# A two-layer decoder step on one core: a fifth row buffer, sample V products over all heads, an operand in PSUM, and attention's preparation moved

## The reference

```python
def swa_sample(xn, ck, cv, w_qkv, b_qkv, w_o, b_o, sinks):
    q, k, v = qkv_proj(xn, w_qkv, b_qkv, qpos)          # with rotary
    kk = jnp.concatenate([ck, k], axis=1)
    vv = jnp.concatenate([cv, v], axis=1)
    o = attend(q, kk, vv, mask, sinks)                  # w = p / denom; o = w @ v
    return o @ w_o + b_o, kk[:, -rows:], vv[:, -rows:]
...
x = x + mixer(rmsnorm(x)); x = x + hier_moe(rmsnorm(x))
...
bbar_r = coef_r * br - coef_i * bi                      # s5_mix, per group of channels
bbar_i = coef_r * bi + coef_i * br
```

## Time and profile before

| | before |
|---|---|
| timed runs, median | 990.99 us (990.83 to 991.28, 3 runs) |
| profiled execution: its time, its span | 988.24, 986.5 |
| mean granted clock of TensorE | 0.866 |
| busy in the span: TensorE, VectorE | 747.4 (76%), 415.8 (42%) |
| busy in the span: ScalarE, GpSimd | 260.2 (26%), 153.5 (16%) |

### The profile page before, as it was taken

How to read it: one execution, slowest core, us unless ns; L and a number is a source line. 1 busy time by engine, 2 the same in 40 slices (tenths; PEclk the granted TensorE clock), 3 DMA queues, 4 the chain that set the end, 5 groups by cost and what they waited for, 6 DMA issues and landing times.

```text
span 986.5 us, 12287 instructions
## 1 busy us (share of the span) xinstructions
PE 747.4 (76%) x4643; PEld 451.5 (46%) x4643; DVE 415.8 (42%) x1002; ACT 260.2 (26%) x554; POOL 153.5 (16%) x218
## 2 busy tenths in 40 slices
PE   4899948999899535998740369989999935998640
PEld 2344426758545333554420257644445524555420
DVE  3478684827578751211115485701111252111118
ACT  6120016616111101332112145520023321222113
POOL 1010000000796401332110112000000001232110
PEclk9999977959999756999985589989999955999995
DMA  9461117000504495999949566592040192999946
GB/s 347 138 197 57 48 59 252 2 1 2 190 21 171 165 401 220 405 410 408 398 137 409 107 127 184 110 364 101 1 170 22 56 390 91 400 410 410 403 161 239
DMA packets 74803, 201.77 MB, mean 205 GB/s; under 512 B 14808, under 2 KB 29528, under 8 KB 73688
## 3 DMA queue, kind: packets, MB, share of 16 engines
q1 hardware_dynamic: 57784, 161.77, 45.4%
q0 software_dynamic: 9696, 19.75, 5.8%
q10 hardware_dynamic: 7264, 19.46, 5.3%
HBM read 171.64 MB, written 39.39 MB: 214 GB/s over the span
## 4 chain that ended last, share of the span: by engine, by line
PE 52%; DVE 15%; DMA 14%; SPq 8%; ACT 6%; issue 4%; POOL 0%; PEldq 0%; POOLq 0%; DVEq 0%; ACTq 0%; PEld 0%
PE PSUM L1995 13%; PE PSUM L1592 9%; PE PSUM L1803 8%; SPq L459 5%; DMA XNT<-in_moe_w_up 4%; DMA PH<-y_scratch 3%; PE PSUM L1823 3%; DMA RING<-in_attn_w_qkv 2%; PE PSUM L1791 2%; SPq L465 2%; PE PSUM L1673 2%; DVE XNT L734 2%; PE PSUM L1945 2%; PE PSUM L1941 2%; DVE X L1475 2%
## 5 line engine op out<-in xcount | busy, mean ns | idle before, releaser
L1592 PE MATMUL PSUM<-RING,XNT 128*128 128x512 f32 (+2 forms) x256 | 94.5, 567 | 4.1 <-DMA RING<-in_attn_w_qkv 3.4
L632 POOL DMA_INDIRECT PH<-xn_scratch,PH x32 | 32.6, 1020 | 359.0 <-DVEq L1420 249.6
L1995 PE MATMUL PSUM<-PH,XNT 128*128 128x512 f32 (+1 forms) x220 | 88.1, 593 | 0.3 <-PE PSUM L1995 0.3
L1803 PE MATMUL PSUM<-RING,PH 128*64 128x256 f32 x384 | 74.9, 417 | 13.2 <-DMA PH<-in_moe_w_up 6.5
L1803 PE MATMUL PSUM<-PH 128*64 128x256 f32 x384 | 65.3, 402 | 10.8 <-DMA RING<-in_moe_w_up 6.2
L1451 DVE TENSOR_TENSOR PH<-PH,PSUM 128x128 f32<-128x128 f32 x32 | 9.3, 289 | 148.8 <-ACT PH L937 148.8
L1592 PEld LDWEIGHTS PSUM<-RING,XNT 128*128 128x128 f32 (+1 forms) x256 | 40.4, 177 | 53.7 <-issue 47.7
L1750 PE MATMUL PSUM<-RING,PH 128*128 128x512 f32 (+1 forms) x160 | 62.6, 593 | 0.0
L1803 PEld LDWEIGHTS PSUM<-RING,PH 128*64 128x64 f32 x384 | 44.4, 151 | 35.1 <-issue 19.8
L708 ACT ACTIVATE XNT<-X 128x1024 f32<-128x1024 f32 (+1 forms) x25 | 26.4, 1054 | 122.0 <-DVE X L1333 66.4
L1995 PEld LDWEIGHTS PSUM<-PH,XNT 128*128 128x128 f32 (+1 forms) x220 | 36.3, 179 | 47.6 <-issue 47.5
(11 more groups left out here) (371 smaller groups left out, 1360.1 us busy)
## 6 DMA issues: line engine op xcount, KB each, us to landing
RING<-in_moe_w_gate SPq DMA_DIRECT2D x24, 512.0 KB
RING<-in_moe_w_up SPq DMA_DIRECT2D x24, 512.0 KB
PH<-in_moe_w_gate SPq DMA_DIRECT2D x24, 512.0 KB
PH<-in_moe_w_up SPq DMA_DIRECT2D x24, 512.0 KB
RING<-in_moe_w_down SPq DMA_DIRECT2D x24, 512.0 KB
PH<-in_moe_w_down SPq DMA_DIRECT2D x24, 512.0 KB
XNT<-in_moe_w_gate SPq DMA_DIRECT2D x16, 512.0 KB
XNT<-in_moe_w_up SPq DMA_DIRECT2D x16, 512.0 KB
```

What stands on the lines that cost most here:

```text
L632: pool.indirect_dma_start(out=XG[:, i % 2, :], out_offset=None, in_=xn_d[layer], in_offset=bass.IndirectOffsetOnAxis(ap=IDX[:, i:i + 1], a ...
L1592: last = te.matmul(PSUM[lo:hi, b0 + col // 512, col % 512:col % 512 + n], XT[:, c, t * P:t * P + r], RING[:, c // 2, (c % 2) * QKV + col:( ...
L1803: last = te.matmul(PSUM[m * 64:(m + 1) * 64, 2 + i % 2, 0:2 * FF], XGT[:, i % 2, c, m * 64:(m + 1) * 64], gu[:, :, c, :], start=(c == 0), ...
L1995: last = te.matmul(PSUM[p0:p0 + r, 2 * (i % 2) + w, :], XT[:, c, t * P:t * P + r], slot(SLOT[q])[:, (2 * (c % 3) + w) * 512:(2 * (c % 3) + ...
```

## The change

1. The K cache's transposes and copies move from phase 2 to phase 1, into the last tile's turn, ahead of its wait for the rotation. `v_block(7)` comes before the last rotation. `inputs()` moves from VectorE to GpSimd, after phase 1; SyncE stores its result behind the `w_o` loads. VectorE's wait before attention is for the V blocks' stores alone.
2. Sample V products: per sample one instruction over all four heads' probabilities and 256 columns of V (and one for the new tokens), of which `out_scale` takes the heads' own blocks, in 8 products of 32 partitions. They fill banks 6 and 7, and `pv` waits for one scaling more at and behind a sample unit.
3. W blocks: half of BB is copied to PSUM bank 3, twice, and four of the six products read it there. VectorE waits for ScalarE's fourth copy of O first. Blocks come 3, 2, 2, 1, 0 to a tile.
4. `YG` gets a fifth buffer: `rows_back` issues five reads with no wait between; the block loads follow. The coefficient and state loads go before the last expert pairs are done, instead of after. `xn_stored` is one semaphore.

The diff leaves out the moved tiles' places in SBUF, `xn_stored`, and the removal of VectorE's `inputs()`, whose body stands in GpSimd's program now.

```diff
@@ -392,10 +390,6 @@
                              ).then_inc(S(f"vec_out{k % 2}"), 16)
-            sp.wait_ge(S("bb_ready"), 1)
-            sp.dma_start(in_d[:, 0:2 * GP * CH], BBQ.rearrange("p r g c -> p (r g c)")).then_inc(S("bb_out"), 16)
-            sp.dma_start(in_d[:, 2 * GP * CH:], PWRQ.rearrange("p r k g -> p (r k g)")).then_inc(S("bb_out"), 16)
-
...
@@ -489,23 +483,24 @@
                 for t in range(NT):
-                    if layer == 0 and t == 4:
-                        for k in range(4):
-                            ring_load(Q_SSM + k, [(slot(SLOT[Q_SSM + k])[:, 0:BLK_F], blk_d[k])])
-                    if t >= 4:
-                        sp.wait_ge(S("yg_used"), layer * 2 * NT + 2 * (t - 3))
-                    sp.dma_start(YG[t % 4][0:ROWS[t], :, :],
+                    sp.dma_start(YG[t][0:ROWS[t], :, :],
                                  y_d[layer].rearrange("(k n) d -> n k d", k=2)[t * P:t * P + ROWS[t]]
-                                 ).then_inc(S(f"yg_full{t % 4}"), 16)
-
+                                 ).then_inc(S(f"yg_full{t}"), 16)
+
+            sp.wait_ge(S("bb_ready"), 1)
+            sp.dma_start(in_d[:, 0:2 * GP * CH], BBQ.rearrange("p r g c -> p (r g c)")).then_inc(S("bb_out"), 16)
+            sp.dma_start(in_d[:, 2 * GP * CH:], PWRQ.rearrange("p r k g -> p (r k g)")).then_inc(S("bb_out"), 16)
             experts(0)
-            sp.wait_ge(S("ring_free"), Q_SSM)
+            sp.wait_ge(S("ring_free"), Q_M0 + 28)
             sp.dma_start(INS, in_d).then_inc(S("ins_in"), 16)
+            sp.wait_ge(S("ring_free"), Q_M0 + 30)
             for r, src in enumerate((st_re, st_im)):
...
             rows_back(0)
+            for k in range(4):
+                ring_load(Q_SSM + k, [(slot(SLOT[Q_SSM + k])[:, 0:BLK_F], blk_d[k])])
...
@@ -576,7 +571,18 @@
             end_phase(pool, 1)
-
+            pool.wait_ge(S("b_in"), 16 * 4)
+            for k in range(8):
+                pool.tensor_copy(PWRQ[:, :, k, :], PW[:, :, 7 - k, :])
+            pool.tensor_copy(PWRQ[:, :, 8, :], PW[:, :, 8, :])
+            cf = [bc(CF[:, r, :].unsqueeze(2), [P, GP, CH]) for r in range(2)]
+            pool.tensor_tensor(BT1, cf[0], BBI[:, 0], ALU.mult)
+            ch(pool.tensor_tensor(BT2, cf[1], BBI[:, 1], ALU.mult))
+            ch(pool.tensor_tensor(BBQ[:, 0], BT1, BT2, ALU.subtract))
+            pool.tensor_tensor(BT1, cf[0], BBI[:, 1], ALU.mult)
+            ch(pool.tensor_tensor(BT2, cf[1], BBI[:, 0], ALU.mult))
+            ch(pool.tensor_tensor(BBQ[:, 1], BT1, BT2, ALU.add))
+            pool.sem_inc(S("bb_ready"), 1)
...
@@ -838,6 +844,11 @@
             for t in range(NT):
+                if t == 4:
+                    for i in range(NSEQ):
+                        act.wait_ge(S("ck_transposed"), i + 1)
+                        nc.scalar.activation(KCT[:, i, :, :], PSUM[0:64, 4 + i % 2, :].rearrange("p (h k) -> p h k", h=KVH),
+                                             ACT.Copy).then_inc(S("kct_ready"), 1)
...
@@ -861,11 +872,6 @@
             end_phase(act, 1)
-
-            for i in range(NSEQ):
-                act.wait_ge(S("ck_transposed"), i + 1)
-                nc.scalar.activation(KCT[:, i, :, :], PSUM[0:64, 4 + i % 2, :].rearrange("p (h k) -> p h k", h=KVH),
-                                     ACT.Copy).then_inc(S("kct_ready"), 1)
...
@@ -1200,11 +1194,11 @@
                     powers()
-                for k in {0: (0, 1), 1: (2, 3), 2: (4, 5), 3: (6,), 4: (7,)}[t]:
+                for k in {0: (0, 1), 1: (2, 3), 2: (4, 5), 3: (6, 7), 4: ()}[t]:
                     v_block(k)
-            inputs()
             end_phase(dve, 1)
-            dve.wait_ge(S("bb_out"), 32)
+            for b in range(2):
+                dve.wait_ge(S(f"vec_out{b}"), 16 * NB // 2)
...
@@ -1281,8 +1275,11 @@
                 else:
-                    for e in range(2):
-                        ins = ve.tensor_tensor(OD[b][:, :, e * 64:(e + 1) * 64], ps, bc(rd, [P, 4, HD]), ALU.mult)
+                    for hh in range(KVH):
+                        rows = slice(32 * hh, 32 * hh + 32)
+                        own = PSUM[rows, 6:8, :].rearrange("p b (g n) -> p (b g) n", g=2)[:, :, hh * HD:(hh + 1) * HD]
+                        for e in range(2):
+                            ins = ve.tensor_tensor(OD[b][rows, :, e * 64:(e + 1) * 64], own, bc(rd[rows], [32, 4, HD]), ALU.mult)
...
@@ -1313,7 +1310,11 @@
                 pw = [bc(PWRW[:, r, 0:L, g0:g0 + BP].rearrange("p k g -> p g k").unsqueeze(3), [P, BP, L, CH]) for r in range(2)]
-                bv = [bc(BBW[:, r, g0:g0 + BP, :].unsqueeze(2), [P, BP, L, CH]) for r in range(2)]
+                half = PSUM[:, 3, :].rearrange("p (r g c) -> p r g c", r=2, g=GP // 2)
+                if k % 4 == 0:
+                    ch(ve.tensor_copy(half, BBW[:, :, g0:g0 + GP // 2, :]))
+                h0 = g0 % (GP // 2)
+                bv = [bc(half[:, r, h0:h0 + BP, :].unsqueeze(2), [P, BP, L, CH]) for r in range(2)]
...
@@ -1321,10 +1322,10 @@
             dve.wait_ge(S("ins_in"), 16)
+            dve.wait_ge(S("ot_ready"), 4)
             for t in range(NT):
-                if t < 4:
-                    w_block(2 * t)
-                    w_block(2 * t + 1)
+                for k in {0: (0, 1, 2), 1: (3, 4), 2: (5, 6), 3: (7,), 4: ()}[t]:
+                    w_block(k)
...
@@ -1470,9 +1471,9 @@
-                    dve.wait_ge(S(f"yg_full{t % 4}"), 16 * (layer * (2 if t % 4 == 0 else 1) + t // 4 + 1))
+                    dve.wait_ge(S(f"yg_full{t}"), 16 * (layer + 1))
                     for k in range(2):
-                        ve.scalar_tensor_tensor(out=X[0:r, t, :], in0=YG[t % 4][0:r, k, :], scalar=CW[0:r, t, k:k + 1],
+                        ve.scalar_tensor_tensor(out=X[0:r, t, :], in0=YG[t][0:r, k, :], scalar=CW[0:r, t, k:k + 1],
...
@@ -1609,6 +1610,15 @@
                     rr = ROWS[tt]
+                    if tt == 4:
+                        pe.wait_ge(S("qkv_read"), 4)
+                        pe.wait_ge(S("ck_in"), 16)
+                        for i in range(NSEQ):
+                            if i >= 2:
+                                pe.wait_ge(S("kct_ready"), i - 1)
+                            for h in range(KVH):
+                                last = te.transpose(PSUM[0:64, 4 + i % 2, h * P:(h + 1) * P], CK[:, i, h * 64:(h + 1) * 64], IDENT[:, :])
+                            last.then_inc(S("ck_transposed"), 1)
...
@@ -1678,7 +1688,9 @@
                 pe.wait_ge(S("pt_ready_act"), i + 1)
-                if i >= 2:
+                if kind == "s" or i and UNITS[i - 1][0] == "s":
+                    pe.wait_ge(S("o_scaled"), i)
+                elif i >= 2:
...
@@ -1691,23 +1703,13 @@
                         sq = 4 * b + g
-                        for hh in range(KVH):
-                            o = PSUM[32 * hh:32 * hh + 32, 6 + i % 2, g * 64:(g + 1) * 64]
-                            te.matmul(o, pt[:, g, 0, 32 * hh:32 * hh + 32], VC[:, sq, hh * 64:(hh + 1) * 64],
-                                      start=True, stop=False)
-                            last = te.matmul(o, pt[0:64, g, 1, 32 * hh:32 * hh + 32], V[0:64, 4, hh * 64:(hh + 1) * 64],
-                                             start=False, stop=True)
+                        o = PSUM[:, 6 + g // 2, (g % 2) * KVD:(g % 2 + 1) * KVD]
+                        te.matmul(o, pt[:, g, 0, :], VC[:, sq, :], start=True, stop=False)
+                        last = te.matmul(o, pt[0:64, g, 1, :], V[0:64, 4, :], start=False, stop=True)
                 last.then_inc(S("pv_done"), 1)
             scores(0)
             scores(1)
-            pe.wait_ge(S("ck_in"), 16)
-            for i in range(NSEQ):
-                if i >= 2:
-                    pe.wait_ge(S("kct_ready"), i - 1)
-                for h in range(KVH):
-                    last = te.transpose(PSUM[0:64, 4 + i % 2, h * P:(h + 1) * P], CK[:, i, h * 64:(h + 1) * 64], IDENT[:, :])
-                last.then_inc(S("ck_transposed"), 1)
             pe.wait_ge(S("kct_ready"), NSEQ)
             pe.wait_ge(S("vc_in"), 16)
             for i in range(NU):

```

More of the change, by code:

```diff
@@ L258, in build @@
         YG1 = XTF[:, 0:4 * D].rearrange("p (b n) -> p b n", b=4)
-        YG = [(YG0 if t < 2 else YG1)[:, 2 * (t % 2):2 * (t % 2) + 2, :] for t in range(4)]
+        YG = [(YG0 if t < 2 else YG1)[:, 2 * (t % 2):2 * (t % 2) + 2, :] for t in range(4)] + [YB]
         RF = RING.rearrange("p k n -> p (k n)")
@@ L453, in experts @@
                         if e == RS + XS + 1:
[L454 removed]
+                            sp.wait_ge(S("xn_stored"), 16 * NT * (layer + 1))
                         if freed(q):
@@ L625, in moe @@
                 pool.wait_ge(S("routed"), layer + 1)
-                pool.wait_ge(S(f"xn_stored{layer}"), 16 * NT)
+                pool.wait_ge(S("xn_stored"), 16 * NT * (layer + 1))
                 n0 = PAIRS * layer
```

26 lines of the change are left out of this document (6 added, 20 removed).

## The result

| | before | changed |
|---|---|---|
| timed runs, median | 990.91 (985.48 to 991.28) | 953.61 (949.2 to 963.55), 4 runs |
| timed again beside other kernels | 988.57 (986.33 to 994.08) | 953.87 (948.07 to 956.43), 4 runs |
| ratio to the runs of before | | 0.9621 [0.9567, 0.9675]; again 0.9635 [0.9595, 0.9675] |
| profiled execution, span | 986.5 | 954.1 |

The kernel is faster, by 35 to 37 us; 948 was forecast, in a range of 939 to 964. Timed runs of either kernel lie 6 to 8 apart. Of the 7.7 between the two traces of the changed kernel 1.4 lie before the first exponential, 1.0 in attention and 6.6 behind GpSimd's copy of the RING rows; the stretches between are 1.3 shorter.

What follows compares the result with a forecast made beforehand. No engine was taken to bound the kernel everywhere; each edit was priced in its stage. 11.3 + 14 + 13 + 4.5 = 42.8 took the profiled time from 988.24 to 945.4; with 2.75 to the timed median, 948, range 939 to 964.

Steps and rivals of the forecast that it cites:

- A: Attention's preparation moved beside the last rotation: unit 0's exponential comes earlier, a gain of 11.3 (9 to 11.8).
- B: Output projection: W blocks with an operand in PSUM relieve VectorE and GpSimd, routing starts earlier; gain 13 (5.6 to 14).
- The rival of no relief: Output projection: a PSUM operand doesn't relieve GpSimd's contention; B gives 5.6, time 955; chance 0.12.
- D: Layer 0's combine: loads moved ahead of the last experts (3) and the fifth row buffer (1.5); gain 4.5 (1 to 8).
- The rival of the whole 10.7: Layer 0's combine: the fifth buffer gives VectorE's whole wait; D gives 13.5, time 939; chance 0.08.
- the share of 1.00: RING row transfer, 541.00 to 554.70: full DMA share at 196 GB/s, taken as evidence against the fifth buffer giving 10.7.
- the rows stay slow wherever they stand: Rows from XNT, layer 0's combine: by the skill's port rule their DMA speed stays low at any queue place; unpriced.
- C: Attention's sample V products as eight merged instructions per unit: 13.3 + 3.5 − 2.7, gain 14 (5 to 15).
- I take the upper level: Sample V products: the granted clock stays at its upper level, so 20.13 becomes 6.86, 13.3 gained.
- rival 1: Attention: the clock falls in the sample units all the same; C gives 5 instead of 14, time 957; chance 0.22.
- the rule of parallel tiles: Sample V products: by the skill's rule 32-column tiles work in parallel, merging loses C's 14, time 962 or later.
- rival 4: Attention: the clock stays at 1.2 GHz throughout, 0.75 lost per microsecond over about 67; slower, 993; chance 0.02.

Runs made afterwards that it cites:

- undo_rows: The changed kernel with four row buffers, block loads ahead of the fifth read, coefficient and state loads behind the experts, as before; 956.45, ratio 0.9659.
- pv_pairs: The changed kernel with the sample V products' same eight instructions reordered, two of 128 rows then two of 64, in two banks by turns; 946.82, ratio 0.9559.
- undo_pv: The changed kernel with the sample V products as before, 32 small instructions per unit, with their scaling and wait; 963.77, ratio 0.976.
- first trace: The first profiled execution of the changed kernel, no edit, slower than its others; span 961.8.
- after2: The changed kernel run again with no edit, for a second trace; 953.87, ratio 0.9635, span 954.1.
- w_sbuf: The changed kernel with the W blocks' BB operand read in SBUF again, block order and wait kept; 956.23, ratio 0.9666.
- blocks_early: The changed kernel with layer 1's four block loads issued right behind layer 0's last expert weights, ahead of the row reads; 947.12, ratio 0.9589.
- undo_w: The changed kernel with the W blocks wholly as before: SBUF operands, old order, no wait for the fourth copy of O; 964.39, ratio 0.9748.
- undo_prep: The changed kernel with attention's preparation as before: K cache transposes, V block 7, inputs() and its stores; 960.59, ratio 0.9704.
- pairs_blocks_state: The changed kernel with paired sample V products, four block loads behind the last expert weights, state loads behind the row reads; 955.38, ratio 0.9682.
- pairs_blocks3: The changed kernel with paired sample V products and three of four block loads behind the last expert weights; 942.69, ratio 0.9533.

## Why the prediction was right, and where it was off

The forecast time and side were right; 42.8 were forecast and 35 to 37 measured. That the sum came so near is in part luck: in B and C the mechanism was another than the one priced. By its own steps:

- **A**, 11.3: 10.2 measured. The start of the rotation and the hidden transposes came as worked out. What was left out of the sum is ScalarE's table load: the exponential was put at 145.9, and there, at 145.98, stands the load of 1.28. GpSimd's products cost 0.9 once, the 1.0 of one wait on the path, where 0.2 was taken; the last copy's end, 141.99 instead of 142.7, makes up for most of it.
- **B**, 13: 10.7. TensorE is the bound after the change, as said, and its projection took the same 68.2. The rest was 11.8 (315.58 to 327.40), not 9.5. But the reason was given to the wrong half: without the PSUM operand 7.0 of the 10.7 remain, by the order of the blocks and its wait. The rival of no relief was priced at a gain of 5.6, and 7.0 is what it would have given; the relief is real (0.68 against 1.61) and worth 3.7.
- **D**, 4.5: 4.0 from the routing to the copy by these two traces, 1.5 to 5.5 by all traces of the same code. The landing itself is 3.0 shorter than before and 3.7 shorter than in undo_rows (3 forecast); for the fifth buffer (1.5 forecast) 0.3 to 0.9 are read, within what traces of the same code differ by. The rival of the whole 10.7 is refuted; the bytes in the queue decided, as the share of 1.00 told. That the rows stay slow wherever they stand isn't borne out: with the blocks ahead of them gone their wait falls from 19.05 to 7.45.
- **C**, 14: 2.4 in the trace, 12 in the timed runs. Three terms were off. 0.43 for an instruction was taken from long ones of equal rows; alternating 128 and 64 rows costs 0.63, 3.2 more over both units. The scaling is waited for 1.26 at each of two places (pv_pairs shows both), where 0.8 was put. And "I take the upper level" is half right: the clock still falls in the sample units or within the next few prompt units, near to what rival 1 said, but how long it stays down now differs from one execution to the next. The table takes the granted clock from 190 to the end of attention, summed over all stretches at the lower level, and the length of attention (first exponential to output projection). Another 10 to 12 at its start are at the lower level in every kernel.

| kernel | lower clock, us | attention, us |
|---|---|---|
| before; undo_pv | 27; 24 | 102.6; 101.1 |
| first trace; after2; undo_rows; w_sbuf | 27; 27; 20; 17 | 101.1; 100.1; 96.8; 97.3 |
| blocks_early; undo_w; undo_prep | 7; 7; 7 | 92.8; 93.0; 92.7 |
| pv_pairs; pairs_blocks_state; pairs_blocks3 | 7; 7; 7 | 91.2; 91.1; 91.3 |

Between 101.1 and 92.7 for the same instructions lie 8.4. That is enough to make one trace of C say 2.4 and the timed runs 12. It isn't all of the scatter of the changed kernel: its own two traces differ by 1.0 here and by 6.6 behind the copy. With the merged products six of these ten traces have 7 at the lower clock, the two with the old ones 24 and 27. At equal 7 the three kernels with pairs take 1.6 less in the mean than the three without, as worked out for them; that they also shorten the lower stretch isn't shown, since three traces could be luck. What in the sample units brings the clock down, the wait for the scaling or the instructions themselves, wasn't separated.

The prediction found the old 32-column products one behind another and took that against the rule of parallel tiles. But tiles of 32 columns do run side by side in this kernel. These are a sample unit's scores (after2, timeline, TensorE):

```profile
170.09 0.44 PE L1668 MATMUL PSUM<-XNT,PH 64*32 64x128 f32 x8
170.33 0.31 PE L1669 MATMUL PSUM<-PH 64*32 64x64 f32 x8
...
171.32 0.36 PE L1669 MATMUL PSUM<-PH 64*32 64x64 f32 x8
...
171.61 1.09 PE L1683 MATMUL PSUM<-IDENT,PH 128*128 128x128 f32 x8
```

Between 170.09 and 171.61 stand 32 records of 128 columns and 32 of 64, 6,144 columns in 1.52; one behind another, at 0.429 for 512, they would take 5.1, an estimate. Scores and old V products both give a tile two instructions and go on to the next. But the scores' two have 64 rows and write to places of their own; the V products' two have 128 and then 64 rows and add up in one place. Which of these keeps the V products apart was not tested, nor whether 32-column products with all those of 128 rows first would have been faster than merged heads.

One sum of the prediction doesn't come out: rival 4's 0.75 for each of 67 is 50, which added to 948 is 998, not 993. Nothing rests on it; the clock was back at its upper level by 162 in all traces with the preparation moved and the sample units in or behind their old places.

## What to carry to other kernels

Read the granted clock of several executions before pricing a stage: here the same code took 92.7 to 101.1, more than most parts of the change were worth, and a single trace of C gave a fifth of its timed worth. When a stage has two engines in series, price the order of the work apart from the speed of its operations; undoing the order cost 7.0, undoing the operand ahead of it 3.7. When a wait in a transfer queue is removed, look for the next bytes in that queue: a fifth buffer gave 0.9 at most of a wait of 10.7, while moving 4.4 to 5.9 MB to where the share was 0.26 to 0.68 gave 4.6 to 4.9 in traces (2.6 to 4.5 in timed runs, which can't tell that from nothing). The pairs and three early blocks together gave the best kernel, 942.69 against 989.23.

## What the runs showed of the hardware that was not expected

- A change between instructions of 128 and 64 rows cost TensorE 0.2 us at 256 columns: 0.63 apiece when they alternate, 1.06 for a pair. At 64 columns it doesn't show: undo_pv's alternate at 0.23, the prompt units' of equal rows follow at 0.22.
- Tiles of 32 columns ran side by side in scores of 64 rows (6,144 columns in 1.52) and one behind another in V products that alternate 128 and 64 rows.
- An operation of 128x4 on VectorE took 1.09 instead of 0.17 while GpSimd's 128x512 product ran, and ended with it. The price is what is left of the other engine's operation, whatever the size of one's own.
- The exponential's table load (1.28) begins when the instruction that needs it is released, though ScalarE had been idle for 3.99.
- A scatter on GpSimd's queue took 9.5 to 11.1 us to land after 4.4 to 5.9 MB of loads had been issued ahead of it on SyncE's, against 3.6 to 4.7; in blocks_early the DMA share was 0.33 at 480 to 485 while it waited. The cause is open.
